# Output projection of a trunk layer: seven block products instead of eight, weight sums kept in memory

## The reference

```python
h = rmsnorm(x, norm1_g)
proj = h @ w_in           # queries, keys, values, indexer, gates
o_a = mixer_a(...)        # attention in a window, with sinks
o_b = mixer_b(...)        # indexer scores, top-k keys per row, attention over them
merged = sigmoid(gate_a) * (o_a @ w_branch_a) + sigmoid(gate_b) * (o_b @ w_branch_b)
x = x + merged @ w_out
h2 = rmsnorm(x, norm2_g)
x = x + (silu(h2 @ w_ffn_gate) * (h2 @ w_ffn_up)) @ w_ffn_down
out = rmsnorm(x, norm_f_g)
```

## Time and profile before

| | us |
|---|---|
| median of 3 runs (3184.79 to 3187.53) | 3185.67 |
| the profiled execution | 3185.86 |
| its span in the trace | 3183.9 |
| PE busy | 3143.7 (99%) |
| POOL busy | 2059.9 (65%) |
| DVE busy | 2005.0 (63%) |
| ACT busy | 1449.8 (46%) |

### The profile page before, as it was taken

One profiled execution on the slowest core, in us unless ns is written; L12 is line 12 of the kernel. 1 busy time (PEld: TensorE's weight loads), 2 busy tenths in 40 slices (PEclk: granted clock), 3 DMA queues, 4 the chain that ended last, 5 costly groups with the idle time before them and its releaser, 6 DMA issues.

```text
span 3183.9 us, 44209 instructions
## 1 busy us (share of the span) xinstructions
PE 3143.7 (99%) x15612; PEld 2643.7 (83%) x15612; DVE 2005.0 (63%) x3889; ACT 1449.8 (46%) x2622; POOL 2059.9 (65%) x2185
## 2 busy tenths in 40 slices
PE   9999999999999999999999999999999999999998
PEld 7888888878888888889888888988888789888887
DVE  3235546537565545557666666967868679647757
ACT  3324445435472534337354543846655368431202
POOL 5666666665556666764666676366666932568778
PEclk9999999999999999999999999999999999999999
DMA  5765455355615333331633334163333411444443
GB/s 154 197 168 172 120 150 161 106 158 164 210 35 182 103 106 108 109 133 35 218 103 108 107 111 139 30 213 116 102 108 105 151 62 21 137 160 127 126 127 101
DMA packets 474699, 401.25 MB, mean 126 GB/s; under 512 B 29905, under 2 KB 405969, under 8 KB 473841
## 3 DMA queue, kind: packets, MB, share of 16 engines
q1 hardware_dynamic: 441072, 342.68, 35.9%
q10 hardware_dynamic: 33408, 55.76, 4.9%
HBM read 332.41 MB, written 62.81 MB: 124 GB/s over the span
## 4 chain that ended last, share of the span: by engine, by line
PE 92%; POOL 3%; ACT 2%; DVE 1%; issue 1%; DMA 1%; POOLq 0%; SPq 0%; ACTq 0%; DVEq 0%
PE BANK L1103 21%; PE BANK L1104 21%; PE BANK L1105 21%; PE BANK L1426 3%; PE LP L1103 3%; PE LP L1104 3%; PE LP L1105 3%; PE BANK L1451 2%; PE LP L1262 2%; PE LP L1261 2%; PE LP L1406 2%; PE LP L1407 2%; PE BANK L1453 2%; POOL WLO L1040 2%; POOL WHI L1038 1%; PE LP L1223 1%
## 5 line engine op out<-in xcount | busy, mean ns | idle before, releaser
L1040 POOL TENSOR_TENSOR WLO<-WRAW,WHI 128x512 fp32r<-128x512 f32 x904 | 1222.7, 1353 | 75.4
L1038 POOL TENSOR_SCALAR WHI<-WRAW 128x512 fp32r<-128x512 f32 x904 | 655.1, 725 | 736.5 <-PE BANK L1105 585.6
L1103 PE MATMUL BANK<-H2hi,WHI 128*128 128x512 f32 x1376 | 539.0, 392 | 1.0 <-POOL WLO L1040 0.9
L1104 PE MATMUL BANK<-H2lo,WHI 128*128 128x512 f32 x1376 | 536.2, 390 | 0.0
L1105 PE MATMUL BANK<-H2hi,WLO 128*128 128x512 f32 x1376 | 536.1, 390 | 0.0
L1103 PE MATMUL BANK<-HThi,WHI 128*128 128x512 f32 (+1 forms) x1024 | 405.4, 396 | 0.8 <-DVE QS L2183 0.5
L1104 PE MATMUL BANK<-HTlo,WHI 128*128 128x512 f32 (+1 forms) x1024 | 399.7, 390 | 0.0
L1105 PE MATMUL BANK<-HThi,WLO 128*128 128x512 f32 (+1 forms) x1024 | 399.5, 390 | 0.0
L1849 ACT ACTIVATE MASK<-SCD,THR 128x896 bf16<-128x896 f32 (+5 forms) x186 | 281.9, 1516 | 190.9 <-DVE THR L2243 164.3
L1105 PEld LDWEIGHTS BANK<-H2hi,WLO 128*128 128x128 f32 x1376 | 258.3, 188 | 54.2
L1103 PEld LDWEIGHTS BANK<-H2hi,WHI 128*128 128x128 f32 x1376 | 258.6, 188 | 53.1 <-issue 1.3
(11 more groups left out here) (356 smaller groups left out, 6552.7 us busy)
## 6 DMA issues: line engine op xcount, KB each, us to landing
WRAW<-in_w_in SPq DMA_DIRECT2D x124, 512.0 KB, 4.3
WRAW<-in_w_ffn_gate SPq DMA_DIRECT2D x88, 512.0 KB, 3.9
WRAW<-in_w_ffn_up SPq DMA_DIRECT2D x88, 512.0 KB, 3.8
WRAW<-in_w_ffn_down SPq DMA_DIRECT2D x81, 512.0 KB, 3.7
qsp<-QS SPq DMA_DIRECT2D x32, 512.0 KB, 5.8
WRAW<-in_w_out SPq DMA_DIRECT2D x32, 512.0 KB, 4.6
gates<-GS ACTq DMA_DIRECT2D x62, 256.0 KB, 2.2
GL<-gates ACTq DMA_DIRECT2D x48, 256.0 KB, 4.0
```

Source lines behind the costliest of these rows:

```text
L1038: nc.gpsimd.tensor_scalar(hi, raw, 1.0, 1.0, ALU.mult, ALU.mult).then_inc(w_hi, 1)
L1040: nc.gpsimd.tensor_tensor(lo, raw, hi.bitcast(f32), ALU.subtract).then_inc(w_split, 1)
L1103: nc.tensor.matmul(dst, whi, mhi, start=first, stop=False)
L1104: nc.tensor.matmul(dst, whi, mlo, start=False, stop=False)
```

## The change

The output projection of all four blocks now goes by seven block products: 7 x 2 x 4 x 3 = 168 matmuls for each block. Only six jobs of w_out per block stay for POOL. The four sums of w_out blocks are formed once, in the projections of blocks 0 and 1, in eight units of six steps (`turn_weights` on ACT, `turn_sums` on DVE: two loads of 256 KB, four subtractions 128x256, a copy and a subtraction 128x1024, two writes of 512 KB), and kept split in memory (`two`). For each block SP loads them back as 16 transfers of 512 KB (TURNED, TW00 to TW33), placed between the jobs of w_out.

DVE writes the merged tiles to SBUF (MEVEN, MODD) instead of leaving them in the bank, and forms their sums (`sum_outs`: SMR, then SMhi on ACT and SMlo on DVE). A branch bank is free when `merged` is set instead of `m_split`. PE takes all four banks for the projection at its start. DVE adds each of the seven products to X as it closes, 14 additions of 128x512 for the 8 of before, and after each of products 0 to 4 makes one search step. PE starts product m (from 2 on) when the additions of product m-2 are made. The half of X that is ready first is now half 1, and it is squared first.

```diff
-            jobs += row_jobs(("wo",), b, io["w_out"][0], range(KT))
+            jobs += [(out_key(b, m, a), every_other(io["w_out"][0], OUT, *RIGHT[m], a))
+                     for m, a in ((0, 0), (0, 1), (3, 0), (3, 1), (5, 0), (5, 1))]
...
+            def load_turned(b, t, ps, i):
+
+                for p in ps:
+                    made(turned_in[i], (b, t, ps), 16)
+                    src = io["two"][:, 4 * TURNED_AT[t] + p].rearrange("h p c -> p h c")
+                    sp.dma_start(TURNED[t][p][:, :, :].bitcast(f32), src).then_inc(turned_in[i], 16)
+
+            def load_all_turned(key, b):
+
+                if key == out_key(b, 0, 1):
+                    if b == 0:
+                        sp.wait_ge(turned_out, n(turned_out, KT - 1))
+                    sp.wait_ge(bank_full, n(bank_full, ("br", b, KT - 1, 0)))
+                    load_turned(b, 0, (0, 1), 0)
+                    load_turned(b, 0, (2, 3), 1)
+                if key == out_key(b, 3, 0):
+                    sp.wait_ge(bank_full, n(bank_full, ("br", b, KT - 1, 1)))
+                    load_turned(b, 1, (0, 1, 2, 3), 2)
+                if key == out_key(b, 3, 1):
+                    sp.wait_ge(merged, n(merged, (b, KT - 1)))
+                    load_turned(b, 2, (0, 1, 2, 3), 3)
+                if key == out_key(b, 5, 1):
+                    sp.wait_ge(bank_full, n(bank_full, out_key(b, 2)))
+                    load_turned(b, 3, (0, 1), 0)
+                    load_turned(b, 3, (2, 3), 1)
...
-                    dst = take("bank" if m or s else "low", *((m_split, (b, m + c)) if s else (gated, (b, m + c, s))),
+                    dst = take("bank" if m or s else "low", *((merged, (b, m + c)) if s else (gated, (b, m + c, s))),
                                ("br", b, m + c, s))
...
+            def seven_out(b, between):
+
+                def left(kind, p):
+                    if type(kind) is int:
+                        pe.wait_ge(sum_low, n(sum_low, (b, "out", p)))
+                        return SMhi[:, p, kind, :], SMlo[p // 2][:, p % 2, kind, :]
+                    m = 2 * p + (kind in ("a12", "a22"))
+                    pe.wait_ge(m_split, n(m_split, (b, m)))
+                    c = slice(2 * P, 4 * P) if kind in ("s3", "a22") else slice(0, 2 * P)
+                    return MGhi[:, m, c], MGlo[:, m, c]
+
+                def right(t, p):
+                    ps, i = ((0, 1, 2, 3), t + 1) if t in (1, 2) else ((0, 1), 0) if p < 2 else ((2, 3), 1)
+                    pe.wait_ge(turned_in[i], n(turned_in[i], (b, t, ps)))
+                    return TURNED[t][p][:, 0, :], TURNED[t][p][:, 1, :]
+
+                seven_products(b, ("wo",), OUT, "bank", left, right, lambda m: out_key(b, m, 0), between)
...
 
-                rows(("wo",), b, MGhi, MGlo, range(KT), m_split, between=lambda: turn(0))
...
+            def turn_weights(u, phase):
+
+                p, c = u // 2, slice(u % 2 * 2 * P, (u % 2 + 1) * 2 * P)
+                if phase == 0:
+                    if u:
+                        act.wait_ge(turned_out, n(turned_out, u - 1))
+                    made(t_in[0], ("out", u), 32)
+                    for h in range(2):
+                        src = io["w_out"][0, (2 * p + h) * P:(2 * p + h + 1) * P, :].rearrange("p (d c) -> p d c", d=2)[:, :, c]
+                        act.dma_start(PRE[:, 2 * h:2 * h + 2, :], src).then_inc(t_in[0], 16)
+                if phase == 3:
+                    act.wait_ge(sum_made, n(sum_made, ("out", u, 2)))
+                    nc.scalar.copy(PREhi[:, :, :], PRE[:, :, :]).then_inc(sum_hi, made(sum_hi, ("out", u)))
+                if phase == 5:
+                    act.wait_ge(sum_low, n(sum_low, ("out", u)))
+                    made(turned_out, u, 32)
+                    for h, t in ((0, PREhi), (1, PRElo)):
+                        dst = io["two"][h].rearrange("(t k) p c -> k p t c", k=4)[p][:, :, c]
+                        act.dma_start(dst, t[:, :, :].bitcast(f32)).then_inc(turned_out, 16)
...
-                    nc.scalar.copy(MGhi[:, m, :], bank(("br", b, m, 1))[:, :]).then_inc(m_hi, made(m_hi, (b, m)))
+                    if m % 2 == 0:
+                        act.wait_ge(sum_made, n(sum_made, (b, "out", m, 3)))
+                        nc.scalar.copy(MGhi[:, m, :].rearrange("p (h r) -> p h r", h=2), MEVEN[:, 0:2, :]
+                                       ).then_inc(m_hi, made(m_hi, (b, m)))
+                    else:
+                        nc.scalar.copy(MGhi[:, m, :].rearrange("p (h r) -> p h r", h=2), MODD[:, :, :]
+                                       ).then_inc(m_hi, made(m_hi, (b, m)))
+                        act.wait_ge(sum_made, n(sum_made, (b, "out", m, 2)))
+                        nc.scalar.copy(SMhi[:, m // 2, :, :], SMR[m // 4][:, m // 2 % 2, :, :]
...
                 for j in range(JT):
-                    square(("wo",), 0, j)
+                    square(("wo",), 1, j)
...
+            def turn_sums(u):
+
+                dve.wait_ge(t_in[0], n(t_in[0], ("out", u)))
+                for to, x, y in ((0, 1, 0), (1, 3, 1), (3, 3, 0), (2, 2, 3)):
+                    if to:
+                        dve.wait_ge(sum_made, n(sum_made, ("out", u, {1: 0, 3: 1, 2: 3}[to])))
+                    nc.vector.tensor_tensor(PRE[:, to, :], PRE[:, x, :], PRE[:, y, :], ALU.subtract
+                                            ).then_inc(sum_made, made(sum_made, ("out", u, to)))
...
+                def sum_outs(m):
+
+                    dve.wait_ge(merged, n(merged, (b, m)))
+                    raw = SMR[m // 4][:, m // 2 % 2, :, :]
+                    for k, to, x, y, op in (((3, MEVEN[:, 1, :], MEVEN[:, 0, :], MEVEN[:, 2, :], ALU.subtract),) if m % 2 == 0 else
+                                            ((0, raw[:, 0, :], MEVEN[:, 2, :], MODD[:, 1, :], ALU.add),
+                                             (1, raw[:, 1, :], raw[:, 0, :], MEVEN[:, 0, :], ALU.subtract),
+                                             (2, raw[:, 2, :], MODD[:, 0, :], raw[:, 1, :], ALU.subtract))):
+                        if k in (1, 2):
+                            dve.wait_ge(sum_made, n(sum_made, (b, "out", m, k - 1)))
+                        nc.vector.tensor_tensor(to, x, y, op).then_inc(sum_made, made(sum_made, (b, "out", m, k)))
+                    dve.wait_ge(sum_made, n(sum_made, (b, "out", m, 2 if m % 2 else 3)))
 
...
+                    whole = MODD[:, :, :] if m % 2 else MEVEN[:, 0:3:2, :]
+                    nc.vector.tensor_tensor(whole, bk[:, :].rearrange("p (h r) -> p h r", h=2),
+                                            M1[:, m % 2, :].rearrange("p (h r) -> p h r", h=2), ALU.add).then_inc(merged, made(merged, (b, m)))
+                    sum_outs(m)
                     dve.wait_ge(m_hi, n(m_hi, (b, m)))
-                    nc.vector.tensor_tensor(MGlo[:, m, :], bk[:, :], MGhi[:, m, :].bitcast(f32), ALU.subtract
+                    nc.vector.tensor_tensor(MGlo[:, m, :].rearrange("p (h r) -> p h r", h=2), MODD[:, :, :] if m % 2 else MEVEN[:, 0:2, :],
+                                            MGhi[:, m, :].bitcast(f32).rearrange("p (h r) -> p h r", h=2), ALU.subtract
                                             ).then_inc(m_split, made(m_split, (b, m)))
+                    if m % 2:
+                        low, raw = (t[m // 4][:, m // 2 % 2, :, :] for t in (SMlo, SMR))
+                        dve.wait_ge(sum_hi, n(sum_hi, (b, "out", m // 2)))
+                        nc.vector.tensor_tensor(low, raw, SMhi[:, m // 2, :, :].bitcast(f32), ALU.subtract
+                                                ).then_inc(sum_low, made(sum_low, (b, "out", m // 2)))
...
+                def add_product(stage, before, m, jj, added):
+
+                    i, d = INTO[m]
+                    j = 2 * i + jj
+                    dve.wait_ge(bank_full, n(bank_full, closed_key(b, stage, m, jj)))
+                    if (d, j) in added:
+                        dve.wait_ge(rows_added, n(rows_added, added[d, j]))
+                    elif before is None:
+                        dve.wait_ge(x_in[j], n(x_in[j], ("again", b)))
+                    else:
+                        dve.wait_ge(rows_added, n(rows_added, (b, before, d, j)))
+                    added[d, j] = added_key(b, stage, m, jj)
+                    c = X1[:, j, d * ROWS:(d + 1) * ROWS]
+                    nc.vector.tensor_tensor(c, bank(("seven", b, stage, PLACE[m], jj))[:, :], c, ALU.add
+                                            ).then_inc(rows_added, made(rows_added, added[d, j]))
...
-                look("wo")
-                for j in range(JT):
-                    add_row(("wo",), None, 0, KT // 2 - 1, j)
-                look("wo", None, 1)
+                added = {}
+                for m in range(5):
+                    for jj in range(2):
+                        add_product(("wo",), None, m, jj, added)
+                    next(found, None)
                 half_mean(("wo",), 1)
```

133 lines of the change are left out of this document (83 added, 50 removed).

## The result

The changed kernel takes 3270.72 us (median of four runs, 3267.62 to 3273.97) against 3185.72 of the kernel before (3184.79 to 3187.53): a ratio of 1.0266, 95% interval 1.0248 to 1.0284, or 85 us more. The forecast was 3253.5, range 3200 to 3285. The profiled execution has a span of 3269.6 us.

A forecast was written before the change was run, and what follows sets the result against it. PE, busy 99% of the span, bounds the kernel, with DVE trailing it at the projection. Blocks 0 to 3 lose 11.8, 20.0, 26.8 and 9.0, together +67.6 on 3185.9: 3253.5 us, range 3200 to 3285.

The forecast's parts named there:

- S: Start of the output projection's first matmul: 5, 9.2, 9 and 9 us after the last branch matmul in blocks 0-3.
- Removed, 21.8 us: Output projection: 24 of 192 matmuls gone in each block, saving 5.44 us a block, 21.8 us in all.
- the ring: Branch stage, gate load to gate load through DVE's sums and ACT's cast: 12 us per row-tile pair against PE's 10.88.
- The short and the long subtraction: Branch stage: DVE's 128x256 subtraction takes 0.42 to 1.5 us; by POOL contention alone S would be at its upper end.
- X reloads: Projection: the first addition needs X reloaded by ACT, taken as 2 us late in every block.
- Search: DVE's search steps between the projection's additions delay product 4: steps 1 to 4 take 15.5, 18.8, 24.0 us in blocks 0-2.
- Clock: Half clock after PE stops: 3.5 us for a stop before S, 2.5 more at turn(0) in blocks 0 to 2.
- Weight sums: nothing: Projections: eight units of added DVE operations and a copy cost nothing; 1 us a unit should banks empty later.
- The other signs: PE idle before the projection least in block 0; DVE without pauses in the branch stage; loss least in block 3.
- DVE keeps up: Rival: new DVE operations run at their short side, X is in time, clock holds; +24, 3210 us; chance 0.20.
- Everything stretches: Rival: S at its upper ends, X 5 us late, both clock drops in full; some +98, 3284 us; chance 0.10.
- The faster one: Rival: search does not bind, PE gets its 21.8 us and pays only for S; 3180 us, or 3164; chance 0.08.

The follow-up runs named there:

- early X: Changed kernel with out<-X issued at m=4 instead of m=6 and the X reloads before ACT's copy of merged tile 7: 3274.9 us.
- early gates: Changed kernel with ACT's gate loads of tile m+2 issued before the cast SMhi instead of behind it: 3262.2 us.
- Half the loads: Changed kernel loading only the high parts of the weight sums, which PE reads in place of the low parts too: 3261.2 us.
- search first: Changed kernel with search steps 1 and 2 before product 0's additions, 3 to 5 after products 1 to 3, ACT's last counts before its squares: 3252.0 us.

## Why the prediction was right, and where not

The direction and the range held, and so did the mechanism: DVE and ACT can't follow PE at this place. The total was 17 us short. Its nearness is partly luck, since the terms missed by more, in both directions: the branch stage (18.8 us) and the weight sums (13.5) were too small, what follows S up to `turn(0)` (11.1) and the clock behind it (3.1) too large.

- *Removed, 21.8 us.* Right, and seen where nothing else is in the way: 38.5 us from S to `turn(0)` in block 3 of the run with early X, 3.7 less than before. The granted clock was 0.77 in the 8 us behind S there, 1.8 us lost, so the forecast's 36.7 would have been met at full clock.
- *S.* The first wait, released by the merge, is where it was expected, but S is 11.6 us late in block 0 and 12.7 to 13.5 in the others, against 5 and 9. In block 0 the ring was the right one, mis-sized in one member: the gate load. I took 3.4 us for it from the earlier trace rows behind a 0.9 us cast; it took 5.8 us from the cast's start at 977.75, with none of the new loads under way, and 6.5 from that at 1004.32, behind four of them. The run with early gates settles it for block 0. In blocks 1 to 3 it was the wrong ring: DVE did not wait for a gate load in the first two rounds, and `finish_rows`, taken as half covered by that load, 1.5 us, stood uncovered in DVE's queue at 3.66 and 3.83 us in block 1. Cutting it to two columns took 4.5 to 7.3 us off.
- *The short and the long subtraction.* Both forms occur, and the long ones beside POOL; but with the gate loads early they fit into PE's 10.88 us in block 0. That S would come at the upper end by this alone is not what happened there; for blocks 1 to 3 no run tells it apart.
- *X reloads.* X cost 0 to 1.5 us, not 2. The loads of the sums, which I had counted as X's company alone, were late themselves, at product 2: 4.1 to 4.7 us in blocks 1 to 3, in block 3 against a forecast of no wait behind S. Half the loads takes that away.
- *Search.* The place was right (XH released `turn(0)`, 1.0, 2.9 and 7.5 us in blocks 0 to 2, none in block 3; search first removes all), the size too large: forecast, with X and the clock, 46.5, 50.8 and 57.5 us from S, measured 40.8, 47.8 and 52.5. In block 0 the steps took 11.7 us instead of 15.5, since I read their lengths from a stretch where POOL stretched the small operations. The wait before product 6 in block 2 did not come: product 2's stop came first, and with half the loads it was product 4 that waited.
- *Clock.* 3.1 us behind the long stop of block 0, but about 1.7 behind those of 4.4 and 4.9 in blocks 1 and 3, so 3.5 was too much there. Behind `turn(0)` it was 0, 1.7 and 1.5 us in blocks 0 to 2, not 2.5.
- *Weight sums: nothing.* This step failed, 13.5 us. I looked at how busy DVE and ACT were the earlier trace rows, and not at what stands behind a DMA issue in ACT's queue, although two issues and a wait were among the steps. That PE stops in the projections had been named as what would prove the prediction wrong, and by that sign it was.
- *The other signs.* PE's idle before the first projection matmul was to be least in block 0; it was largest there, 10.0 us against 4.4 to 5.0, because in blocks 1 to 3 PE had already stopped for 4.9 us inside the branch stage. DVE was to have no pauses there; in block 0 it waited 3.2 and 3.4 us for GL. The loss was to be least in block 3; it was least in block 0 (10.8 against 15.6), since product 2 waited in block 3 as well.
- *The rivals.* DVE keeps up (3210) is closest to block 0 of the early-gates run, and needed an edit. Everything stretches (3284) is a little nearer in time than the forecast, and right on S, which is past its upper end in block 0 and near it in the others; X 5 us late and the clock drops in full did not come. The faster one wanted block 2's stretch at 36.7 us; search first brought it to 44.9.

## What to carry over

When a step is moved to an engine's queue, count its DMA issues and waits as work of that queue, and ask which instruction behind them another engine needs: here one cast in front of a gate load, itself waiting for DVE, cost 8.4 us in block 0, and the loads and writes of the weight sums most of 13.5, though ACT had been busy 29 us in 100 there and DVE 35 before they were added. Read the length of a small operation from a stretch whose neighbours are as busy as they will be; a busy share does not tell it. Fewer matmuls pay only where PE is the last to finish, and this stage was one where DVE trailed PE already.

## What the runs showed that I had not expected

- A single DMA issue can hold the issuing queue for long: a write of the weight sums 3.36 us of ACT's, a load of them 7.63 of SP's at 1584.51, where the shortest took 0.4. The loads of that set on SP, with the DMA engines at some 400 GB/s:

```profile
1583.77 12.07 SPq L874 DMA_DIRECT2D TW<-two  x4
```

- The four X reloads take 1.96 us of ACT's queue in block 0 and are spread over 6.12 in block 1. There each issue takes only 0.3 to 0.4 us; between them ACT waits until out<-X of the same rows has landed.
- Operations of 128x4 on DVE took 0.16 us in some places and 0.8 to 1.2 us in others, the long ones ending with a POOL subtraction that ran beside them.
- Most stops of PE cost twice: behind those at S, at product 2 and at `turn(0)` of blocks 1 and 2, the granted clock stood at 0.50 for some us, worth 1.4 to 3.1 us more. But not all: in the 8 us behind the stops of 2.43 us at 101.64, of 2.53 at 887.05 and of 1.01 at 1057.36 it stayed at 1.00. The second of these stands at the same place of the program as the one in the earlier trace rows, which was followed by 0.50.
